# Neighbourhood attention by pairs of heads on half arrays, with the bias added by VectorE

## The reference

```python
def _na_context(h, ...):          # 128 context tokens read one another
    s = jnp.einsum('bhqd,bhkd->bhqk', q, k) * (C_DH ** -0.5)
    p = jax.nn.softmax(s, axis=-1)
    o = jnp.einsum('bhqk,bhkd->bhqd', p, v)
    return (o * jax.nn.silu(g)) @ w_out, k, v

def _na_latent(h, k_ctx, v_ctx, ...):   # per row of the grid
    # 16 columns of every one of the 4 rows around the query, with a learned bias, and 128 cached tokens
    s_loc = jnp.einsum('bhqd,bhrqwd->bhqrw', q_r, k_w) * scale + bias[None]
    s_ctx = jnp.einsum('bhqd,bhcd->bhqc', q_r, k_ctx) * scale
    p = jax.nn.softmax(jnp.concatenate([s_loc, s_ctx], axis=-1), axis=-1)
    return einsum(p_loc, v_w) + einsum(p_ctx, v_ctx)
```

## Time and profile before

| | us |
|---|---|
| runs, median (lowest to highest of 3) | 1951.94 (1946.57 to 1952.37) |
| profiled execution, span from its first to its last instruction | 1948.8 |
| median of the runs above that span | 3.1 |
| layer C from the first scores to the first matmul of its output projection | 1181.6 to 1337.8, that is 156.2 |

### The profile page before, as it was taken

The page is one execution under the profiler, slowest core; times in us unless marked ns, Lnnn a source line. Parts: engine busy times, 40 slices in busy tenths (PEclk is TensorE's granted clock), DMA queues, the critical chain, the costliest instruction groups (busy, mean ns, idle before and its releaser), DMA issues.

```text
span 1948.8 us, 16614 instructions
## 1 busy us (share of the span) xinstructions
PE 1816.9 (93%) x6421; PEld 1050.9 (54%) x6421; DVE 604.2 (31%) x979; ACT 495.2 (25%) x960; POOL 167.7 (9%) x158
## 2 busy tenths in 40 slices
PE   6899999999989899988989998999799998898998
PEld 3355534755655554546455455545455536575655
DVE  0333005336340202375320552321433005445420
ACT  2201323323320114343111222231201223433300
POOL 1000001001000000052043000000100001100100
PEclk9999998999999998999999997999899999999999
DMA  6522222233242321242365221323222221212122
GB/s 189 203 86 86 88 74 76 76 112 116 83 146 95 113 86 43 76 150 98 130 126 156 86 86 44 98 98 110 73 86 87 99 74 44 83 48 87 44 88 75
DMA packets 105140, 185.98 MB, mean 95 GB/s; under 512 B 5136, under 2 KB 54704, under 8 KB 105072
## 3 DMA queue, kind: packets, MB, share of 16 engines
q1 hardware_dynamic: 95816, 158.40, 24.2%
q0 software_dynamic: 8640, 26.46, 4.6%
q10 hardware_dynamic: 616, 0.16, 0.1%
HBM read 164.47 MB, written 20.54 MB: 95 GB/s over the span
## 4 chain that ended last, share of the span: by engine, by line
PE 88%; DVE 5%; ACT 3%; issue 1%; DMA 1%; SPq 0%; DVEq 0%; ACTq 0%; POOLq 0%
PE acc L500 69%; PE mix L500 17%; PE acc L565 1%; DMA out_new_C<-cst 1%; DVE hT L1523 1%; ACT cp L1276 1%; DVE mix L1344 1%; DVE rd L1505 1%; DVE cstat L1666 1%; PE mix L915 0%; DMA ring<-in_a_w_out 0%; DMA cst<-in_c_k_g 0%; DVE dx L1590 0%; DVE hT L1348 0%; DVE fqk L1626 0%
## 5 line engine op out<-in xcount | busy, mean ns | idle before, releaser
L500 PE MATMUL acc<-hT,ring 128*128 128x385 f32 x1664 | 548.3, 491 | 15.8 <-DVE hT L1351 14.4
L500 PEld LDWEIGHTS acc<-hT,ring 128*128 128x128 f32 x1664 | 317.9, 192 | 244.6 <-issue 21.9
L500 PE MATMUL acc<-z,ring 128*128 128x385 f32 x512 | 169.5, 492 | 6.1 <-DMA ring<-in_a_w_out 4.2
L500 PE MATMUL acc<-ring,sc 128*2 128x384 f32 x512 | 170.2, 486 | 1.6 <-ACT mst L992 1.2
L500 PEld LDWEIGHTS acc<-z,ring 128*128 128x128 f32 x512 | 97.9, 192 | 77.7 <-issue 6.1
L500 PE MATMUL mix<-qs,ring 128*128 128x256 f32 x512 | 117.6, 392 | 9.6 <-DVE qs L1507 9.6
L500 PEld LDWEIGHTS mix<-qs,ring 128*128 128x128 f32 x512 | 100.1, 197 | 27.6 <-issue 13.2
L500 PEld LDWEIGHTS acc<-ring,sc 128*2 128x2 f32 x512 | 41.3, 85 | 119.1 <-issue 112.2
L1363 DVE SCALAR_TENSOR_TENSOR y<-acc,modv,y 128x128 f32 x64 | 23.4, 413 | 223.8 <-PE acc L500 223.8
L500 PE MATMUL acc<-ring,hT 128*128 128x512 f32 x192 | 85.5, 608 | 0.0
L500 PE MATMUL acc<-xc,bd 128*128 128x385 f32 x128 | 57.5, 574 | 14.2 <-DVE hT L1523 8.4
(11 more groups left out here) (297 smaller groups left out, 2212.6 us busy)
## 6 DMA issues: line engine op xcount, KB each, us to landing
ring<-in_w_mod SPq DMA_DIRECT2D x64, 768.0 KB, 6.2
ring<-in_a_w_in SPq DMA_DIRECT2D x32, 1024.0 KB, 6.9
ring<-in_state_mlstm_C SPq DMA_DIRECT2D x16, 1024.0 KB, 7.8
out_new_C<-cst POOLq DMA_DIRECT2D x32, 512.0 KB, 3.2
ring<-in_a_w_out SPq DMA_DIRECT2D x16, 1024.0 KB, 7.8
ring<-in_c_w_in SPq DMA_DIRECT2D x16, 1024.0 KB, 7.6
ring<-in_b_w_in SPq DMA_DIRECT2D x12, 1024.0 KB, 6.3
ring<-in_b_w_out SPq DMA_DIRECT2D x4, 1024.0 KB, 6.2
```

The source lines that it names most:

```text
L500: return nc.tensor.matmul(out, lhsT=lhsT, rhs=rhs, start=start, stop=stop)
```

## The change

The loop runs over pairs k of heads. `scores(k)` issues the scores of both heads, alternating matmul by matmul between head 2k on partitions 0 to 63 and head 2k+1 on partitions 64 to 127; the two heads' scores go to two separate pairs of banks (`PAIR * e`). The two identity matmuls for the bias are gone; `maxima(h)` on VectorE adds the bias in place in PSUM, two additions of 128 by 256 per head. `values(k)` alternates likewise between the two heads, which write the two halves of the output partitions. `cp` and `cpt` have four buffers instead of two; the new two lie in `cqr` and `ckrt`, which nothing reads any more at this point. Waits are per pair where they were per head: `scores(k + 1)` waits for the exponentials of both heads of pair k. The wait for the finished bias moves from TensorE to VectorE.

```diff
-                def scores(h):
-                    k, r = h // 2, slice(64 * (h % 2), 64 * (h % 2) + 64)
-                    if h:
-                        pe.wait_ge(cx_ready, h)
-                    mm(mix[:, 0:P], cq3[r, k, 0:P], ck3[r, k, 0:P], True, True)
-                    for q in (1, 2):
-                        ps = mix[:, seg(q * 512, TC)]
-                        qt = cq3[r, k, seg(TOK[q], P)]
-                        mm(ps[:, 0:NLAT], qt, ck3[r, k, LAT:W], True, False)
-                        mm(ps[:, 0:NLAT], ident[:, :], cb4[:, q - 1, h, :], False, True)
-                        ins = mm(ps[:, NLAT:TC], qt, ckc[r, k * P:(k + 1) * P], True, True)
+                def scores(k):
+                    if k:
+                        pe.wait_ge(cx_ready, 2 * k)
+                    for c, n, t, keys in ((0, P, 0, ck3[:, k, 0:P]),
+                                          (P, NLAT, 1, ck3[:, k, LAT:W]), (TC, P, 1, ckc[:, k * P:(k + 1) * P]),
+                                          (512, NLAT, 2, ck3[:, k, LAT:W]), (768, P, 2, ckc[:, k * P:(k + 1) * P])):
+                        for e in range(2):
+                            r = head_rows(e)
+                            ins = mm(mix[:, seg(PAIR * e + c, n)], cq3[r, k, seg(TOK[t], P)], keys[r, :], True, True)
                     ins.then_inc(cs_ready, 1)
...
+                    for b in range(3):
+                        for e in range(2):
+                            h = 2 * k + e
+                            hv = slice(h * CDH, (h + 1) * CDH)
+                            v = cvc[:, hv] if b == 2 else cv3[:, 1 + b, hv]
+                            both = cpt[h % 4][:, P:896].rearrange("p (q b t) -> p q b t", q=2, b=3)[:, :, b, :]
+                            ins = mm(ps[head_rows(h), P:TC].rearrange("p (q t) -> p q t", q=2), v, both, b == 0, b == 2)
...
-                for h in range(CH):
-                    if h + 1 < CH:
-                        scores(h + 1)
-                    turn(h)
-                    if h:
-                        values(h - 1)
-                    if h and h % 2 == 0:
-                        mod_part(l + 1, h // 2 - 1)
-                values(CH - 1)
+                for k in range(KD):
+                    if k + 1 < KD:
+                        scores(k + 1)
+                    turn(2 * k)
+                    if k:
+                        values(k - 1)
+                    turn(2 * k + 1)
+                    if k:
+                        mod_part(l + 1, k - 1)
+                values(KD - 1)
...
+                exps(0)
+                exps(1)
+                for k in range(KD):
+                    turned(2 * k)
+                    if k + 1 < KD:
+                        exps(2 * k + 2)
+                    turned(2 * k + 1)
+                    if k + 1 < KD:
+                        exps(2 * k + 3)
+                    if k:
+                        mod_part(l + 1, k - 1)
...
                 def maxima(h):
...
+                    for q in range(2):
+                        s = mix[:, seg(at + P + q * TC, NLAT)]
+                        ins = tt(s, s, cb4[:, q, h, :], ALU.add)
+                    link(ins)
...
+                for k in range(KD):
+                    normalise(2 * k)
+                    normalise(2 * k + 1)
+                    if k + 1 < KD:
+                        maxima(2 * k + 2)
+                        maxima(2 * k + 3)
+                    if k:
+                        gated(k - 1)
```

More of the change, by code:

```diff
@@ L54 @@
 MC = 3 * D // MOD_CHUNKS
+PAIR = 1024
 SLOTS = 2
@@ L124, in sem, with seg @@
             return ctx.enter_context(nc.semaphore(name))
+        def seg(col0, n=None):
+            return slice(col0, col0 + n)
         acc = [ctx.enter_context(nc.psum_tensor(f"acc{b}", [P, 512], F32))[:, :] for b in range(2)]
@@ L255, in trunk @@
             knt = sb("knt", D, stack=st)
-            cp = [sb(f"cp{s}", 896, stack=st) for s in range(2)]
-            cpt = [sb(f"cpt{s}", 896, stack=st) for s in range(2)]
+            cp = [sb(f"cp{s}", 896, stack=st) for s in range(2)] + [cqr[:, seg(896 * s, 896)] for s in range(2)]
+            cpt = [sb(f"cpt{s}", 896, stack=st) for s in range(2)] + [ckrt[:, seg(896 * s, 896)] for s in range(2)]
             cst_ = [sb(f"cstat{s}", 6, stack=st) for s in range(2)]
@@ L381, in rmstile @@
             return tile("rms", l, h) if h < BH - 1 else tile("rms3", l)
-        def seg(col0, n=None):
-            return slice(col0, col0 + n)
         block = ctx.enter_context(nc.Block())
@@ L894, in natten, with head_rows @@
                         (lambda ps, e=e: ps[:, e * P:(e + 1) * P], ck3[:, 4 * n + e, 0:P]) for e in range(4)])
-                def scores(h):
-                    k, r = h // 2, slice(64 * (h % 2), 64 * (h % 2) + 64)
-                    if h:
-                        pe.wait_ge(cx_ready, h)
-                    mm(mix[:, 0:P], cq3[r, k, 0:P], ck3[r, k, 0:P], True, True)
-                    for q in (1, 2):
-                        ps = mix[:, seg(q * 512, TC)]
-                        qt = cq3[r, k, seg(TOK[q], P)]
-                        mm(ps[:, 0:NLAT], qt, ck3[r, k, LAT:W], True, False)
-                        mm(ps[:, 0:NLAT], ident[:, :], cb4[:, q - 1, h, :], False, True)
-                        ins = mm(ps[:, NLAT:TC], qt, ckc[r, k * P:(k + 1) * P], True, True)
+                def head_rows(h):
+                    return slice(CDH * (h % 2), CDH * (h % 2) + CDH)
+                def scores(k):
[7 more added lines that the diff above has]
+                            ins = mm(mix[:, seg(PAIR * e + c, n)], cq3[r, k, seg(TOK[t], P)], keys[r, :], True, True)
                     ins.then_inc(cs_ready, 1)
@@ L914, in turn @@
                     for b in range(7):
-                        ins = nc.tensor.transpose(mix[:, seg(3 * 512 + b * P, P)], cp[h % 2][:, b * P:(b + 1) * P],
+                        ins = nc.tensor.transpose(mix[:, seg(2 * PAIR + b * P, P)], cp[h % 4][:, b * P:(b + 1) * P],
                                                   ident[:, :])
                     ins.then_inc(ct_ready, 1)
[L919 to L933, removed]
@@ new lines, in values @@
+                def values(k):
+                    pe.wait_ge(cpt_ready, 2 * k + 2)
+                    ps = bank(tile(f"attn{k}", l))
+                    for e in range(2):
+                        h = 2 * k + e
+                        mm(ps[head_rows(h), 0:P], cv3[:, 0, h * CDH:(h + 1) * CDH], cpt[h % 4][:, 0:P], True, True)
+                    for b in range(3):
+                        for e in range(2):
+                            h = 2 * k + e
+                            hv = slice(h * CDH, (h + 1) * CDH)
+                            v = cvc[:, hv] if b == 2 else cv3[:, 1 + b, hv]
+                            both = cpt[h % 4][:, P:896].rearrange("p (q b t) -> p q b t", q=2, b=3)[:, :, b, :]
+                            ins = mm(ps[head_rows(h), P:TC].rearrange("p (q t) -> p q t", q=2), v, both, b == 0, b == 2)
+                    ins.then_inc(acc_ready, 1)
@@ L1272, in exps @@
                     act.wait_ge(mx_ready, h + 1)
-                    if h >= 2:
-                        act.wait_ge(ct_ready, h - 1)
+                    if h >= 4:
+                        act.wait_ge(ct_ready, h - 3)
                     for q, (c, n) in enumerate(((0, P), (P, TC), (P + TC, TC))):
-                        ins = nc.scalar.activation(cp[s][:, seg(c, n)], mix[:, seg(q * 512, n)], ACT.Exp,
+                        ins = nc.scalar.activation(cp[h % 4][:, seg(c, n)], mix[:, seg(PAIR * s + c, n)], ACT.Exp,
                                                    bias=cst_[s][:, q:q + 1], accum_out=cst_[s][:, 3 + q:4 + q])
@@ L1281, in turned @@
                     act.wait_ge(ct_ready, h + 1)
[L1282 to L1290, removed]
+                    if h >= 4:
+                        act.wait_ge(acc_ready, tile(f"attn{h // 2 - 2}", l) + 1)
+                    nc.scalar.copy(cpt[h % 4], mix[:, seg(2 * PAIR, 896)]).then_inc(cpt_ready, 1)
+                exps(0)
[9 more added lines that the diff above has]
+                        mod_part(l + 1, k - 1)
                 mod_part(l + 1, KD - 1)
@@ L1663, in maxima @@
                     st_ = cst_[h % 2]
-                    dve.wait_ge(cs_ready, h + 1)
-                    for q, n in enumerate((P, TC, TC)):
-                        ins = nc.vector.tensor_reduce(st_[:, q:q + 1], mix[:, seg(q * 512, n)], AX, ALU.max)
+                    at = PAIR * (h % 2)
+                    dve.wait_ge(cs_ready, h // 2 + 1)
+                    for q in range(2):
+                        s = mix[:, seg(at + P + q * TC, NLAT)]
+                        ins = tt(s, s, cb4[:, q, h, :], ALU.add)
+                    link(ins)
+                    for q, (c, n) in enumerate(((0, P), (P, TC), (P + TC, TC))):
+                        ins = nc.vector.tensor_reduce(st_[:, q:q + 1], mix[:, seg(at + c, n)], AX, ALU.max)
                     link(ins)
```

(8 more changed lines are left out.)

1 line of the change is left out of this document (removed).

## The result

The changed kernel takes 1894.32 us (1892.62 to 1896.50, 4 runs) against 1951.20 us for the kernel before on the same chip: ratio 0.9715, 95% interval 0.9699 to 0.9730. That is 57 us less, where 48.8 were forecast (1903, range 1894 to 1916).

What follows compares the result with a forecast made beforehand. TensorE, busy 93% of the span, was taken as the bound. With rounds of 11.10 us for 18.04, the stage falls from 156.2 to 107.4, 48.8 us less: 1900.0 against the profiled span, 1903 against the median; range 1894 to 1916.

Steps and rivals of the forecast that it cites:

- likeliest case: Whole kernel: half arrays overlap, TensorE bounds the pair; 1903 us, own range 1897 to 1908, chance 0.78.
- favourable case: Stage from first scores: both kinds of halves overlap perfectly, clock back by 24; stage some 102 us, time 1898.
- TensorE bounds the stage: Steady rounds: TensorE's work sets a pair with its `w_mod` part, 11.10 us in place of 18.04.
- Halves overlap: Two heads side by side on TensorE's half arrays: a pair's scores 2.0 us, values 1.75.
- slip: Pair's scores: if matmuls start only in queue order, alternating ones slip by one record, giving 2.0 us.
- The bias: VectorE: two additions of 128 by 256 per head, 0.41 us each, far ends 0.35 and 1.7.
- rival (c): VectorE becomes the bound at 1.7 us per addition: loop 13.4 us, stage 126, time 1922; chance 0.05.
- The waits at the start: First two pairs: TensorE waits for both heads' maxima and exponentials, uncovered by `w_mod`; first wait 6.2 us.
- The clock: Stage start: 1.2 GHz level for 19 us after work resumes, until about 27 us into the stage.
- Rival (d): TensorE's clock stays low longer; if for the whole stage, stage 186 us, time 1982; chance 0.03.
- Four buffers: Buffers of probabilities and turned probabilities: claimed to cost nothing themselves.
- The cover of 0.7 us on the projection's weights: Stage end: 2 MB weight chunk takes 7.8 us to move, with 8.5 us between issue and use.

Runs made afterwards that it cites:

- bias on VectorE alone: Kernel before with only the bias moved to VectorE, heads one by one, two buffers, no alternating: 1937.71 us, ratio 0.9948 (0.9932 to 0.9965).

## Why the prediction was right, point by point

- *The number.* 1894.3 lies at the lower edge of the stated range (1894), and below the 1897 to 1908 of the likeliest case: that it is inside is luck by a few tenths. The stage was put at 107.4 and took 101.2; its favourable case (full overlap, clock back by 24, 102) is what came. The 2.9 us outside the stage were not forecast.
- *TensorE bounds the stage and a round becomes its work.* Right: 10.75 against 11.10 forecast, and doubling VectorE's additions does not move it.
- *Halves overlap.* Right, and more fully than taken. Scores were put at 2.0 between 1.7 and 3.4, for a slip of one record if matmuls must start in order. They took 1.73, the lower bound; values 1.67 against 1.75. The slip does not exist, and it is the largest mis-sized term: about 2.8 us of the stage, 0.27 in each of five rounds and 1.5 in the first three pairs. The two starts of the earlier trace rows already spoke against it for columns; I kept it for rows. The Trainium skill (TensorE: Matmul & The Clock Gate, Part 3) has matmuls strictly in order; in the run with scores head by head, three records of the first head were still to run when the second head's first one started.
- *The bias.* 0.423 us against 0.41, in the lower part of a range up to 1.7; rival (c) is out. The Trainium skill (TensorEngine Tiling (Array Packing), Performance Considerations) warns that emptying PSUM may become the bottleneck; in the steady rounds TensorE never waits for it, and at the start it waits 6.1 and 3.2 us.
- *The waits at the start.* The first took 6.13 us against 6.2. For the second I had both heads' additions and maxima one after the other ahead of the copy and the exponential, 7.2 us from scores to scores. The second head's ran beside the first head's exponentials, and it took 1196.79 - 1190.59 = 6.2: 1 us less.
- *The clock.* Mis-sized as well. I gave it 19 us to come back, as before; it came back in 3.4, and fell once more, for 3.4, behind the second wait. That made the third pair's scores, the transposes behind them and the first values about 2 us shorter than forecast. With the slip and the second wait this is the 4.6 us by which the first `w_mod` part began earlier (1203.70 - 1179.35 = 24.4 us into the stage instead of 29.0); the rounds behind it give 1.8, and the end takes 0.3 back: 6.2 in all. What returned the clock early is the order of the scores: in the run with the same work head by head it took 20 us. Rival (d) is out: from 1203.6 the clock holds 1.00 to the end of the stage.
- *Four buffers "cost nothing".* True, but they are also worth something that the sum did not name: 1.15 us of wait in each round without them.
- *The cover of 0.7 us on the projection's weights.* It was used up: a wait of 0.5 us. It cost almost nothing, for 0.47 us of waiting for ScalarE stood there before.

Undone one at a time from the changed kernel, the stage grows by 19.2 (bias), 11.7 (alternating scores), 8.4 (buffers) and 5.5 us (alternating values); the bias done alone on the kernel before takes 14.6 us off its stage. These do not add up to the 55.0 of the whole: each is measured with the other parts in place.

## What to carry to other kernels

Two half-height or half-width matmul streams ran here in the time of one when they alternated in the queue; put one after the other they shared only the last three records. Moving work off the bound engine pays in full only where something covers the longer loop that it makes: the same bias move saved 2.5 us in every round inside pairs; without them it left TensorE a wait of 1.35 us, saved 2.5 in the first such round and 0.9 in the five in which the clock fell behind the wait. When a wait at the start of a stage is left, look for independent matmuls whose weights are already fetched; here they saved the wait and the low clock behind it.

## What the runs showed of the hardware

Two matmuls of the two row halves take no longer together than one: a pair's 20 score records run in 1.73 us, where one head's ten alone take 1.74 (bias on VectorE alone). Overlap across the order of the queue reached three records, for rows and for columns alike. After a long wait TensorE's granted clock returned to 1.00 within 3 to 6 us of work when the scores alternated (five runs). With one head at a time it took 13 us (bias on VectorE alone), 19 (the kernel before) and 20 (scores head by head), and in these three it returned during or just behind the first values. The run with scores head by head differs from the changed kernel in the order of the scores alone, so by these two profiles the order decides; how it does so is not shown. A wait of TensorE of 1.35 us in each round was followed by a fall of the clock in five rounds of six, at 1.7 us each (bias on VectorE alone); one of 1.15 us in each of seven rounds was not (two buffers). What separates the two cases is open.
